# Attention input projection: the rotary half swap's pieces issued by ScalarE, its products one tile later, own buffers for the keys

## The reference, cut to what matters

```
px = hx @ w_in                                   # 512 x 1024 by 1024 x 1536
qx = rope(rms_norm(px[..., :1024] per head, q_g))
kx = rope(rms_norm(px[..., 1024:1280] per head, k_g)); vx = px[..., 1280:]
_rotate_half(part): concatenate([p1 * cos - p2 * sin, p2 * cos + p1 * sin])
```

## Time and profile before

| | us |
|---|---|
| median of three runs | 2731.26 |
| profiled execution | 2734.78 |
| its span | 2733.1 |
| TensorE busy | 2622.0 (96% of the span) |
| VectorE busy | 1623.6 (59%) |
| ScalarE busy | 957.8 (35%) |
| mean granted TensorE clock | 0.98 |

### The profile page before, as it was taken

How to read it: one execution, slowest core, us unless ns; L and a number is a source line. 1 busy time by engine, 2 the same in 40 slices (tenths; PEclk the granted TensorE clock), 3 DMA queues, 4 the chain that set the end, 5 groups by cost and what they waited for, 6 DMA issues and landing times.

```text
span 2733.1 us, 36001 instructions
## 1 busy us (share of the span) xinstructions
PE 2622.0 (96%) x13764; PEld 2170.9 (79%) x13764; DVE 1623.6 (59%) x2536; ACT 957.8 (35%) x1405; POOL 96.1 (4%) x185
## 2 busy tenths in 40 slices
PE   7999998999999988999999999989999989899997
PEld 6888887888888877568888888878888878788886
DVE  4877646454556544664755565776556776644446
ACT  2323523222212232664422334353232353532224
POOL 0000000000000000000000000000000000000000
PEclk9999998999999989999999999999999999999998
DMA  6342322333334313001445554234546522233332
GB/s 242 123 137 83 119 79 70 108 108 107 111 111 131 115 53 87 16 1 46 148 146 165 166 184 135 77 95 141 173 144 188 170 81 78 78 93 94 98 94 85
DMA packets 85195, 306.06 MB, mean 112 GB/s; under 512 B 10448, under 2 KB 12624, under 8 KB 84048
## 3 DMA queue, kind: packets, MB, share of 16 engines
q1 hardware_dynamic: 59008, 209.45, 24.5%
q0 software_dynamic: 26064, 94.91, 11.2%
HBM read 299.60 MB, written 2.10 MB: 110 GB/s over the span
## 4 chain that ended last, share of the span: by engine, by line
PE 87%; DVE 6%; ACT 3%; issue 2%; DMA 1%; SPq 1%; DVEq 0%; ACTq 0%
PE G L447 20%; PE G L449 20%; PE G L448 20%; PE G L474 5%; PE G L475 5%; PE G L476 5%; PE B L640 2%; SPq L392 1%; PE G L849 1%; PE B L889 1%; PE G L523 1%; PE G L524 1%; PE G L525 1%; DVE X L1740 1%; PE B L865 1%
## 5 line engine op out<-in xcount | busy, mean ns | idle before, releaser
L995 ACT ACTIVATE Whi<-Wraw 128x1024 fp32r<-128x1024 f32 x357 | 375.0, 1051 | 498.8 <-DMA Wraw<-wstream_dram 482.2
L1482 DVE TENSOR_TENSOR Wlo<-Wraw,Whi 128x1024 fp32r<-128x1024 f32 x357 | 436.3, 1222 | 143.1 <-ACT Whi L995 142.3
L447 PE MATMUL G<-h_hi,Whi 128*128 128x512 f32 (+1 forms) x1040 | 371.1, 357 | 2.8 <-DVE Wlo L1482 2.8
L448 PE MATMUL G<-h_lo,Whi 128*128 128x512 f32 (+1 forms) x1040 | 368.1, 354 | 0.0
L449 PE MATMUL G<-h_hi,Wlo 128*128 128x512 f32 (+1 forms) x1040 | 368.1, 354 | 0.0
L447 PE MATMUL G<-hs_hi,Whi 128*128 128x512 f32 x768 | 306.4, 399 | 2.6 <-DVE Wlo L1482 1.7
L449 PE MATMUL G<-hs_hi,Wlo 128*128 128x512 f32 x768 | 303.3, 395 | 0.0
L448 PE MATMUL G<-hs_lo,Whi 128*128 128x512 f32 x768 | 303.3, 395 | 0.0
L449 PE MATMUL G<-hid_hi,Wlo 128*128 128x512 f32 (+1 forms) x792 | 290.6, 367 | 0.0
L447 PE MATMUL G<-hid_hi,Whi 128*128 128x512 f32 (+1 forms) x792 | 290.6, 367 | 0.0
L448 PE MATMUL G<-hid_lo,Whi 128*128 128x512 f32 (+1 forms) x792 | 290.6, 367 | 0.0
(11 more groups left out here) (387 smaller groups left out, 4383.1 us busy)
## 6 DMA issues: line engine op xcount, KB each, us to landing
Wraw<-wstream_dram SPq DMA_DIRECT2D x357, 512.0 KB, 3.6
Araw<-adaw_dram POOLq DMA_DIRECT2D x180, 512.0 KB, 4.0
FIRST<-firstw_dram SPq DMA_DIRECT2D x4, 1536.0 KB, 23.4
X<-xin_dram SPq DMA_DIRECT2D x4, 1536.0 KB, 11.6
SWAP<-T SPq DMA_DIRECT2D x64, 32.0 KB, 2.0
out_dram<-X SPq DMA_DIRECT2D x16, 128.0 KB, 1.7
ROW<-rows_dram SPq DMA_DIRECT2D x2, 768.0 KB, 6.1
CB<-cvec_dram SPq DMA_DIRECT2D x2, 512.0 KB, 5.4
```

Source lines behind the costliest of these rows:

```text
L447: pe.matmul(o, wh, hi[:, a:b], start=(k == 0), stop=False)
L448: pe.matmul(o, wh, lo[:, a:b], start=False, stop=False)
L995: act.activation(Whi[:, t % 4, :], Wraw[:, t % 4, :], ACT.Copy).then_inc(w_hi, 1)
L1482: dve.tensor_tensor(Wlo[:, t % 4, :], Wraw[:, t % 4, :], Whi[:, t % 4, :].bitcast(F32), ALU.subtract).then_inc(w_lo, 1)
```

## The change

SP no longer issues any swap; it only streams weights. ScalarE issues the eight pieces of the swap itself. For query tile n it does so right behind its own copy into `T`, after waiting for that copy, in round t = n + 2. In round 4 this stands ahead of the square root of key 1's norm. The swaps of keys 0 and 1 stand in rounds 5 and 6, between `split_hi` and the rest of the round, each behind a wait for the key (`qk_n`). The keys get buffers 2 and 3 of `SWAP`, with semaphores of their own. VectorE turns the tile of round t-1 in round t, not that of round t-2; in round 6 it turns key 1 and queries 2 and 3. `qk_turn(9)` stays where it is.

```diff
-        SWAP = sb("SWAP", [P, 2, NX], where=p5)
+        SWAP = sb("SWAP", [P, 4, NX], where=p5)
-        swapped = [sem(f"swapped{i}") for i in range(2)]
+        swapped = [sem(f"swapped{i}") for i in range(4)]
@@ sync
-            def swap_halves(n):
-
-                if n < 2:
-                    sp.wait_ge(qk_n, n + 1)
-                else:
-                    sp.wait_ge(tile_free[(T_ATT + 2 + n) % 2], (T_ATT + 2 + n) // 2 + 1)
-                wait(sp, qk_ready, n - 1)
-                x_ = (QN if n < 2 else T)[:, n % 2, NC:NT]
-                for g in range(0, P, 16):
-                    sp.dma_start(SWAP[g:g + 16, n % 2, :], x_[g ^ 16:(g ^ 16) + 16, :]).then_inc(swapped[n % 2], 16)
-
-            for t in range(4, N_ATT + 3):
-                load(At(T_ATT + t))
-                for n in {7: (0,), 8: (1, 2), 9: (3, 4)}.get(t, (t - 5,) if t > 9 else ()):
-                    swap_halves(n)
-            stream(T_ATT + N_ATT + 3, T_S)
+            stream(T_ATT + 4, T_S)
@@ scalar
+            def swap_halves(n):
+
+                x_, s = (QN, 2 + n) if n < 2 else (T, n % 2)
+                for g in range(0, P, 16):
+                    act.dma_start(SWAP[g:g + 16, s, :], x_[(g ^ 16):(g ^ 16) + 16, n % 2, NC:NT]).then_inc(swapped[s], 16)
+
             for t in range(N_ATT):
-                evac(At(T_ATT + t))
+                if t in (5, 6):
+                    split_hi(At(T_ATT + t + 2))
+                    act.wait_ge(qk_n, t - 4)
+                    swap_halves(t - 5)
+                    wait(act, tile_done, At(T_ATT + t + 1))
+                else:
+                    evac(At(T_ATT + t))
...
                         act.activation(T[:, n % 2, a:b], ps(g, a, b), ACT.Copy, scale=small[:, 0:1]).then_inc(
                             tile_free[(T_ATT + t) % 2], 1)
+                        freed(act, At(T_ATT + t))
+                        swap_halves(n)
@@ vector
-                dve.wait_ge(swapped[n % 2], 128 * (n // 2 + 1))
-                link(dve.tensor_tensor(dst, SWAP[:, n % 2, :], ROPE[:, 1, :], ALU.mult))
+                s = 2 + n if n < 2 else n % 2
+                dve.wait_ge(swapped[s], 128 if n < 2 else 128 * (n // 2))
+                link(dve.tensor_tensor(dst, SWAP[:, s, :], ROPE[:, 1, :], ALU.mult))
...
+                if t == 6:
+                    qk_turn(2)
                 if t >= 6:
-                    qk_turn(t - 4)
-            qk_turn(8)
+                    qk_turn(t - 3)
```

## The result

The changed kernel takes 2741.37 us at the median of 7 runs (2738.91 to 2745.78), the kernel before 2732.01 us (2730.35 to 2733.66). That is 9.4 us more; the ratio is 1.0036, with a 95% interval from 1.0024 to 1.0047. The forecast was 8 us more, by ScalarE's order. The profiled execution of the changed kernel has a span of 2741.0 us, 7.9 more than before.

A forecast was written before the change was run, and what follows sets the result against it. SP's issue time bound the attention input; -15.1 us for removed stalls, turned into +7.0 by ScalarE's batches, plus 1.0 for collisions, gave +8 us on 2731.3: 2739.3 us. Forecast's own range 2736.5 to 2744 (chance 0.42); wide range 2716 to 2744.

The forecast's parts named there:

- The 15.1 us: Attention input: the most the change can bring, 8.9 us of TensorE idle and 6.2 of low clock.
- The price of a piece: ScalarE's issue time for swap pieces, taken as SP's: 4.94 us per batch of eight, 0.6175 from piece to piece.
- rivals 1 to 3: ScalarE's issue costs next to nothing (-15, chance 0.17), as SP's plain loads (-11.2, 0.16), or between (-5 to +3, 0.19).
- Rival 2: A piece costs ScalarE what plain loads cost on SP, 0.37 us: -11.2 us, 2720; chance 0.16.
- Rounds 4 to 6: Four batches between tile 4's copy into `T` and tile 6's `SQ` put that `SQ` at 1060.0; TensorE idles some 7.5 us.
- The rounds after: Steady ScalarE rounds to tile 11: 7.21 us each against TensorE's 6.47, so `SQ` of tile 11 comes 5.3 us later.
- The tail: After `SQ` of tile 11, swap 9 puts `QR` 6.2 us behind it, was 2.55; first maximum 7.0 us late.
- collisions: SP's loads lengthen ScalarE's batches if both queues can't issue at once: 0 to 2.9 us over five rounds, taken as 1.
- rival 4: Forecast's mechanism and more: key pieces wait for `Whi`, or a piece each round takes 1640 ns: +10 to +16 us; chance 0.06.
- Part 3: VectorE's turn moved by one tile and the keys' own buffers: hides with 3.7 us to spare, cost 0.

The follow-up runs named there:

- pool_issues: Changed kernel with all 80 swap pieces issued by GpSimd, none by ScalarE or SP: 2718.0 us, 0.9941 of the kernel before.
- sp_old_order: Changed kernel with all pieces issued by SP in the kernel before's order, key buffers and earlier turn kept: 2727.1 us, 0.9981 of the kernel before.
- half_each: Changed kernel with four pieces of each swap issued by ScalarE, four by SP behind the load of tile n+6: 2723.8 us, 0.9966 of the kernel before.
- pool_late_turn: All pieces on GpSimd, but VectorE turns each query tile two rounds later, as in the kernel before: 2718.3 us, 0.9936 of the kernel before.
- behind_whi: Changed kernel with each query batch one step later in ScalarE's order, behind the next weight tile's upper split: 2737.7 us, 1.0016 of the kernel before.

## Why the prediction was right

- **The bound and what it was worth.** The 15.1 us read as idle (8.9) and low clock (6.2) were there: pool_issues shortens the stretch by 14.9, with 0.1 us of idle left and a granted clock of 1.00. One reading of the earlier trace rows was loose. The load issued at 1067.76 belongs to the tile after the 3.24 us stall. The load that this stall waited for went out at 1060.97, behind two batches (before, SP's timeline, columns as in rows 3):
```profile
1050.94 9.98 SPq L392 DMA_DIRECT2D SWAP<-T  x16
1060.97 0.58 SPq L355 DMA_DIRECT2D Wraw<-wstream_dram  x1
```
  The conclusion is the same, that pieces held up the loads. For the first stall (1.70 us) it is not: its turn waited for the pieces themselves and not for a load, and it stays in sp_old_order.
- **The price of a piece.** It was the open number, bounded from a few tens of ns to over 1 us and taken from SP's rows: 4.94 us a batch. Measured 5.00 (514 ns alone, 611 in a row), so rivals 1 to 3 fell. The number held; the reason given for it, that equal register operations mean equal DMA issues, was tested by no run. Rival 2 also had the bytes wrong: a weight load carries 512 KB and a piece 32, sixteen times and not eight, which makes its point that bytes don't set the price stronger. The Trainium skill's "usually small relative to the DMA itself" ("DMA: Bandwidth & Descriptors", "Issuing engines are not separate DMA queues") does not hold for these pieces: on ScalarE one is 0.61 us of issue for 2.0 of landing, and the swap's eight together 5.0. The 50 ns of dispatch that the prediction takes from the same page of the Trainium skill stand there under "Anatomy of one DMA — SWDGE (gpsimd) path", that is for a DMA issued by GpSimd; of GpSimd's own pieces pool_issues shows 484 ns each.
- **Rounds 4 to 6.** The square of tile 6 was forecast 28.3 us after that of tile 4 and came at 30.4, with the named wait chain (key 1's landing, its sine product, the turn of query 2). The stall in round 5 was forecast at 1.1 us and is 1.06; that before tile 6 at 7.5 and is 9.46.
- **The rounds after.** Forecast 7.21 us, measured 7.25 to 7.27, with one of 8.20.
- **The tail.** `QR` 6.2 us behind the last square, measured 6.23.
- **The sum.** The stretch was to grow by 7.0 us and 1 more for collisions; it grew by 10.3, and the median by 9.4. The missing 3.3 beside the 7.0 can be read from the trace: two batches with a long piece each (1.58 and 1.36 us, the second with a gap of 0.3; together 1.9 over the usual batch), batches of 5.00 us in place of 4.94 (ten of them, 0.6), and key 1's sine product 2.9 us after its batch, not 2.0 (0.9). That is 3.4; small steps elsewhere give the rest back.
- **The term that was wrong in kind.** The 1 us for collisions between SP's loads and ScalarE's pieces. SP's loads took 333 ns at the most while ScalarE issued, as they do alone, and the two batches with a load inside and no long piece took 5.00 and 4.99 us (loads at 1044.94 and 1051.29). So this term was nothing. Two queues that both issue pieces do disturb each other, but little: of the Trainium skill's lock wait ("Perfetto Trace Analysis", "DMA Instruction — HWDGE (DVE, Sync)") half_each can hold at most 0.26 us in four pieces. The microsecond in the sum was right by luck, since long pieces filled it; those the prediction had only in rival 4.
- **Part 3 at cost 0** held for the earlier turn (pool_late_turn, where no issue is in the way). For the key buffers it was not tested alone.

## What to carry to other kernels

On ScalarE, a DMA within SBUF of 32 KB and one of 64 KB hold the issuing queue alike, some 0.6 us. So a transfer cut into eight is 5 us in the order of SP or ScalarE, and 3.8 in that of GpSimd. Ask what stands behind it there, for SP (a weight load) as for ScalarE (the next split, square and root). Add a batch to its issuer's round and compare with the bound's round before moving it. The place for such pieces is a queue that has nothing due.

## What the runs showed of the hardware that I had not expected

- A swap piece costs least on GpSimd: 484 ns, with no gap between pieces, against 589 on SP and 611 on ScalarE.
- Single issues take 1.1 to 1.7 us, in each kernel with SP or ScalarE as the issuer (1640 ns before, 1577 and 1365 after). Where one starts, a packet of the instruction queue moves, as at the changed kernel's long piece at 1038.43 (window 1038 to 1040.2: packets, MB, share):
```profile
q8 instruction: 1, 0.02, 3.2%
```
  The same holds for every issue above 1 us in this stretch, in all nine kernels with SP or ScalarE as the issuer: the half microsecond in which it starts, or the one before, has such a packet. Two windows of 3 us without a long piece have none. In pool_issues two such packets fall into the stretch, and no piece takes more than 499 ns. That fetching instructions holds up the issue on SP and ScalarE fits all this, and was not tested.
- A longer stall didn't keep the clock down longer: after 9.46 us of idle the matmuls were at the low level from 1060.57 to about 1065.4, after 3.24 us (before) from 1070.30 to about 1076.9.
- The load of an activation table waits in the sequencer behind DMA issues, though the engine is free: in behind_whi it starts at 1101.04, right behind the batch that began at 1096.01, after 4.72 us in which the engine did nothing.
